# Fourier's first product over half the frequencies, modulation granules in pairs, angle steps in one place, and tensors moved to multiples of 128 bytes

## The reference

```python
mod_l = silu_c @ w_mod[l] + b_mod[l]      # w_mod[l]: 1024 x 3072
mod_c = silu_cc @ w_mod[l] + b_mod[l]
sh_l, sc_l, g_l = jnp.split(mod_l, 3, axis=-1)
h_l = rmsnorm(x, norm_g[l]) * (1 + sc_l[:, None]) + sh_l[:, None]
```

```python
ang = positions.astype(jnp.float32)[..., None] * inv_freq
return jnp.cos(ang), jnp.sin(ang)
```

## Time and profile before

| | us |
|---|---|
| median of 3 runs | 1123.51 |
| lowest, highest | 1123.21, 1123.52 |
| the profiled execution, as a whole | 1121.75 |
| its span (first to last instruction) | 1119.9 |

### The profile page before, as it was taken

The page is one execution under the profiler, slowest core; times in us unless marked ns, Lnnn a source line. Parts: engine busy times, 40 slices in busy tenths (PEclk is TensorE's granted clock), DMA queues, the critical chain, the costliest instruction groups (busy, mean ns, idle before and its releaser), DMA issues.

```text
span 1119.9 us, 15597 instructions
## 1 busy us (share of the span) xinstructions
PE 1086.1 (97%) x5974; PEld 883.6 (79%) x5974; DVE 683.9 (61%) x1198; ACT 554.7 (50%) x999; POOL 77.2 (7%) x94
## 2 busy tenths in 40 slices
PE   7999999999999999999999999999998999999997
PEld 5889776688886988776688778889796678889785
DVE  5986665566545786575566547523256753876664
ACT  5654364455435554364455445334235642534772
POOL 1000110000002000110000000001000002021040
PEclk9999999999999999999999999999999999999999
DMA  9644576665666744486876485223211012443001
GB/s 300 218 141 151 173 241 192 219 211 186 188 188 203 242 139 152 143 280 211 256 235 183 153 323 153 73 87 107 75 58 57 1 57 57 132 142 122 2 1 38
DMA packets 109716, 170.46 MB, mean 152 GB/s; under 512 B 7229, under 2 KB 70730, under 8 KB 109386
## 3 DMA queue, kind: packets, MB, share of 16 engines
q1 hardware_dynamic: 107668, 161.95, 45.8%
q0 software_dynamic: 1440, 6.10, 1.6%
q10 hardware_dynamic: 534, 1.41, 0.3%
HBM read 168.39 MB, written 1.05 MB: 151 GB/s over the span
## 4 chain that ended last, share of the span: by engine, by line
PE 84%; DVE 8%; ACT 4%; issue 3%; DMA 1%; POOL 0%; SPq 0%; DVEq 0%; POOLq 0%; ACTq 0%
PE PS L477 16%; PE PS L478 15%; PE PS L479 15%; PE PS L2997 4%; PE PS L2998 4%; PE PS L2999 4%; PE PS L977 3%; PE PS L1810 1%; DVE low L450 1%; PE PS L941 1%; PE PS L942 1%; PE PS L943 1%; PE PS L1484 1%; ACT high L440 1%; PE PS L1798 1%
## 5 line engine op out<-in xcount | busy, mean ns | idle before, releaser
L450 DVE TENSOR_TENSOR low<-raw,high 128x1024 fp32r<-128x1024 f32 (+3 forms) x182 | 202.2, 1116 | 190.8 <-ACT high L440 189.9
L477 PE MATMUL PS<-high,hT_high 128*128 128x512 f32 (+2 forms) x796 | 308.0, 387 | 4.3 <-DVE low L450 2.0
L478 PE MATMUL PS<-low,hT_high 128*128 128x512 f32 (+2 forms) x796 | 299.5, 376 | 0.0
L479 PE MATMUL PS<-high,hT_low 128*128 128x512 f32 (+2 forms) x796 | 299.4, 376 | 0.0
L440 ACT ACTIVATE high<-raw 128x1024 fp32r<-128x1024 f32 (+3 forms) x186 | 179.6, 972 | 221.1 <-PE PS L479 123.4
L477 PEld LDWEIGHTS PS<-high,hT_high 128*128 128x128 f32 x796 | 150.6, 189 | 49.5 <-issue 15.0
L453 DVE SCALAR_TENSOR_TENSOR low<-raw,vec_cols,high 128x512 fp32r<-128x512 f32 x176 | 124.2, 747 | 75.3 <-ACT high L443 75.2
L479 PEld LDWEIGHTS PS<-high,hT_low 128*128 128x128 f32 x796 | 150.5, 189 | 24.2
L478 PEld LDWEIGHTS PS<-low,hT_high 128*128 128x128 f32 x796 | 150.8, 189 | 21.7
L443 ACT ACTIVATE high<-raw,vec_cols 128x512 fp32r<-128x512 f32 x176 | 117.1, 714 | 73.9 <-PE PS L479 38.5
L2997 PE MATMUL PS<-high,fT_high 128*128 128x512 f32 x176 | 70.4, 400 | 0.0
(11 more groups left out here) (377 smaller groups left out, 1602.0 us busy)
## 6 DMA issues: line engine op xcount, KB each, us to landing
raw<-w_gate_up SPq DMA_DIRECT2D x176, 256.0 KB
raw<-w_mod SPq DMA_DIRECT2D x48, 512.0 KB
raw<-w_down SPq DMA_DIRECT2D x44, 512.0 KB
raw<-w_in SPq DMA_DIRECT2D x56, 384.0 KB
raw<-o_w_in SPq DMA_DIRECT2D x20, 512.0 KB
raw<-w_out SPq DMA_DIRECT2D x16, 512.0 KB
raw<-e_w_in SPq DMA_DIRECT2D x12, 512.0 KB
raw<-w_in SPq DMA_DIRECT2D x8, 512.0 KB
```

Source lines behind the costliest of these rows:

```text
L450: last = e.tensor_tensor(g.low, g.raw, g.high.bitcast(F32), ALU.subtract)
L477: e.matmul(bank, xh[:, k, tokens], g.high[:, i, :], start=first and i == 0, stop=False)
L478: e.matmul(bank, xh[:, k, tokens], g.low[:, i, :], start=False, stop=False)
L479: done = e.matmul(bank, xl[:, k, tokens], g.high[:, i, :], start=False, stop=last and i == len(g.rows) - 1)
```

## The change

Four edits, with no common core.

1. The token matrix keeps 129 of the 256 frequencies (0 to 128), for cosine and sine. The first product is 258 columns wide instead of 512. The copy out of PSUM becomes two: frequencies 0 to 127 as they stand, and 128 to 255 from 128 down to 1, read backwards. The sine part has the wrong sign there, so the second product takes the channel sines with the other sign for the upper tile (a third block of `dft_channels`).
2. `MOD_AT` names two places per chunk, h = 1 and h = 3, with two granules each.
3. The angle steps 5, 1 and 2 all come behind the cut of granule 3.
4. `hT_high` and `hT_low` are declared right behind `low`, and `half_power` is 8 columns wider. By the declared sizes both then start at a multiple of 128, and so does everything from `mixer` on.

```diff
-    parts["dft_tokens"] = by_tile(np.concatenate([np.cos(turn), np.sin(turn)], 1))
+    half = slice(0, SEQ // 2 + 1)
+    parts["dft_tokens"] = by_tile(np.concatenate([np.cos(turn)[:, half], np.sin(turn)[:, half]], 1))
...
-    parts["dft_channels"] = np.concatenate([np.cos(turn), -np.sin(turn)], 1) / np.sqrt(SEQ * P)
+    parts["dft_channels"] = np.concatenate([np.cos(turn), -np.sin(turn), np.sin(turn)], 1) / np.sqrt(SEQ * P)
...
         low = [sb(f"low{i}", [P, SLOT], F32R) for i in range(CUT)]
+        hT_high = sb("hT_high", [P, DK, SEQ], F32R)
+        hT_low = sb("hT_low", [P, DK, SEQ], F32R)
         consts = sb("consts", [P, a["const_early"].shape[1]])
...
-        hT_high = sb("hT_high", [P, DK, SEQ], F32R)
-        hT_low = sb("hT_low", [P, DK, SEQ], F32R)
...
-        half_power = sb("half_power", [P, 16])
+        half_power = sb("half_power", [P, 24])
...
-        MOD_AT = {(2, h): (0, h) for h in range(4)} | {(4, h): (1, h) for h in range(4)}
+        MOD_AT = {(2, 1): (0, 0), (2, 3): (0, 2), (4, 1): (1, 0), (4, 3): (1, 2)}
...
-                        add_mod(layer, 0, (of,), PAIRS[n:n + 1])
+                        add_mod(layer, 0, (of,), PAIRS[n:n + 2])
...
-                    last = e.matmul(PS[:, 4 + i % 4, :], z_late[:, NT * s + t, g * P:(g + 1) * P],
+                    last = e.matmul(PS[:, 4 + i % 4, 0:2 * FH], z_late[:, NT * s + t, g * P:(g + 1) * P],
                                     late_const("dft_tokens", NT)[:, t, :], start=t == 0, stop=t == NT - 1)
...
-                copy(e, mine, fourier_T[:, i, :], PS[:, 4 + i % 4, :]).then_inc(mine.sem, mine.mark(f"fourier{i}"))
+                halves = PS[:, 4 + i % 4, 0:2 * FH].rearrange("p (c n) -> p c n", c=2)
+                to = fourier_T[:, i, :].rearrange("p (c n) -> p c n", c=2)
+                copy(e, mine, to[:, :, 0:P], halves[:, :, 0:P])
+                copy(e, mine, to[:, :, P:SEQ], halves[:, :, P:0:-1]).then_inc(mine.sem, mine.mark(f"fourier{i}"))
...
+                        of = part * (1 + t % NT)
                         rows = slice(part * SEQ + t % NT * P, part * SEQ + (t % NT + 1) * P)
                         last = e.matmul(PS[:, F_BANKS[t], g * P:(g + 1) * P], fourier_T[:, 4 * s + g, rows],
-                                        channels[:, part * P:(part + 1) * P], start=part == 0, stop=part == 1)
+                                        channels[:, of * P:(of + 1) * P], start=part == 0, stop=part == 1)
...
-        EARLY = {0: 5, 1: 1, 2: 2, 4: 3, 6: 4}
+        EARLY = {0: (5, 1, 2), 4: (3,), 6: (4,)}
...
-                    early_dve(e, EARLY[s])
+                    for step in EARLY[s]:
+                        early_dve(e, step)
...
-                        mod_rows_pe(e, 0, of, slice(n, n + 1))
+                        mod_rows_pe(e, 0, of, slice(n, n + 2))
```

More of the change, by code:

```diff
@@ L1472, in program @@
                    for s, banks in enumerate(banks2))
+        FH = SEQ // 2 + 1
         def fourier_first_pe(e):
```

## The result

The changed kernel takes 1095.64 us, the median of four runs (1094.57 to 1096.27). The kernel before, run beside it on the same chip, took 1123.36 (1121.22 to 1123.52). The ratio is 0.9757, with a 95% interval from 0.974 to 0.9773. The forecast was 1106.9 with a range down to 1103.0, so the kernel is 11.3 us faster than forecast and 7.4 us outside the range.

A forecast was written before the change was run, and what follows sets the result against it. PE, busy 97% of the span, bounds the kernel. Savings of 9.36 (modulation pairs), 6.8 (Fourier), 0.44 (angles) and 0 (places) sum to 16.6 us, taken off 1123.51 for 1106.9 us, range 1103 to 1112.

The forecast's parts named there:

- Pairs: Modulation in gate_up: 16 single granules at 1.18 us become 8 pairs at 1.19, saving 9.36 us.
- price of a pair: Two modulation granules together cost PE 1.19 us, read from the last layer's down product; one alone costs 1.18.
- cover of 2.8 us: Slack in gate_up's chunk 3 between a buffer's release and cuts (6.8 us) and PE's use of the granule (9.6).
- "ring late" rival: Weight buffers given back in twos delay loads; half the modulation gain, 4.7 us, is lost, giving 1111.6; chance 8%.
- Fourier: First Fourier product: 32 instructions, each 254 columns narrower at 0.84 ns per column, save 6.8 us; copies cost 0.
- bound of twice the price for a backward read: Fourier's copies: were PSUM twice as slow backwards, DVE's pair would take 1.1 us, under PE's 1.74, costing nothing.
- Angles: Early angle steps fill DVE's idle time, so PE's product after its 2.71 us wait for `qk` starts 0.44 us sooner.
- the 1.4 us of that rival: PE's clock stays up behind the shortened `qk` wait, saving 1.4 us more, giving 1105.5; chance 27%.
- the wait of 2.02 us: A PE wait elsewhere in the earlier trace without a clock fall, cited as a sign the clock may stay up.
- Places of the tensors: Operand places in rounded products: rows show no dependence on place, so gain 0, with 0.233 us from start to start.
- every rounded product gets faster: Aligned operands cut rounded products from 0.457 to 0.417 ns per column, 20 ns per 512 columns, near 1045 us; chance 5%.
- Slower than before: Streaming and stationary operands at the same offset make reads meet; at 10 ns per 512-column product, 1133 us; chance 2%.

The follow-up runs named there:

- e2_no_places: The changed kernel with the new places of the tensors undone, so pairs, 129 frequencies and early angles alone: 1106.93 us beside 1122.82 for the kernel before, ratio 0.9859.
- e1_places: The kernel before with only the new tensor places added (`hT_high`, `hT_low` behind `low`, `half_power` wider): 1111.51 us beside 1122.82, ratio 0.9903.
- e11_fourier512: The changed kernel with all 256 frequencies in the first product and one copy per unit again: 1101.66 us beside 1122.11 for the kernel before.

## Why the prediction was wrong

**Pairs: right, and the ring a little late.** The sum of 9.36 holds (9.44 seen), and with it the price of a pair. But PE has one new wait for a low part, of 0.4 to 1.7 us, in every trace with pairs but those with the constants later. The prediction had named such a wait as a sign of being wrong, but looked for it in another place. Its cover of 2.8 us was worked out for the second granule of the chunk behind a pair (chunk 3), and PE doesn't wait there. The late granule is the second of chunk 4, whose load stands in SP's queue behind the next pair. And the forecast had counted the buffers and not the other loads: a large one on POOL's queue falls into the same stretch, in the second layer only. The "ring late" rival was right in kind at 1.7 of its 4.7 us.

**Fourier: right.** 0.217 per product and 6.8 us, copies at nothing. The bound of twice the price for a backward read wasn't needed: it takes 0.41 us where a forward one takes 0.42.

**Angles: the size right, the place not.** 0.4 to 0.5 for the 0.44, and ACT's table load was indeed late next. But the prediction took the 0.44 off the wait of 2.71 and expected 2.3. The wait is 2.64; five sixths of the gain lie at the product near 41 us that no longer comes late. The clock fell in this trace; behind the same wait it stayed up in others (granted 1.00 in e2_no_places), so the 1.4 us of that rival belong to every kernel here, before included. The prediction also leaned on the wait of 2.02 us in the earlier trace rows that isn't followed by a fall. In 5 of the 17 traces that same wait is.

**Places of the tensors: wrong, and the whole miss.** The time from start to start, which the prediction had named as its sign, went from 0.233 to 0.227. The step that failed says that "the costs would have to agree by accident", and concluded 0. It compared 397 ns (512 columns) with 280 (256 columns), took the 0.457 ns per column between them as the price of a column, and argued that a misplaced operand couldn't be in it, as it is the streaming one in the first and the stationary one in the second. But what counts is the distance between the two, and that was 32 bytes in both rows (with the roles exchanged), so comparing them could say nothing about it. The misplacement even had opposite signs in the two, and both went into the slope: it made 512 columns 6 ns longer and 256 columns 3 ns shorter. After the change the same two rows give (391 - 283) / 256 = 0.422 ns per column. The 0.04 ns above a cycle at 2.4 GHz, which the prediction saw and took for a property of the type, was the misplacement.

The rows of before could have warned. Here they are for the three widths, with the group of 384 that the prediction didn't use, groups by shape of the kernel before:

```profile
L478 PE MATMUL PS<-low,hT_high 128*128 128x384 f32 x252 | 85.3, 339 | 0.0
```

280, 339 and 397 lie on one line of 0.457 ns per column. Those are durations, whose ends are modelled. From start to start the same three take 118, 174 and 234 ns, steps of 56 and 60 for 128 columns each; after the change they take 120, 174 and 227, steps of 54 and 53. So the starts, which the prediction used elsewhere, put 512 columns off the line. No product of `high` or `low` with `hT`, `fT` or `cT` has a distance of 0 in the kernel before, so its trace couldn't say that the place was free. The words "no dependence on place" were read from rows in which the good place never occurred. The bounds for this step were 0 and the 20 ns per product of the rival, and the chance of 5% was too low for the only explanation it had of a slope above a cycle.

**The rival "every rounded product gets faster"** had the right mechanism in its slope (0.417 against the 0.422 seen) and the wrong size: 53 us and 10 more, where the kernel gained 11.3. It took the fixed part of a product as unchanged. By the durations it rose as the slope fell: 280 - 256 x 0.457 = 163 ns before, 283 - 256 x 0.422 = 175 after. So 256 columns lose 3 ns, 384 stay about even (339 to 337), and only 512 win, 6 ns in 397. The 2,592 such products by 5.6 ns (the mean spacing went from 233.2 to 227.6) are 14.5 us. About 1.0 of it is taken by the 256-column products (408 by 2.4 ns), 0.3 lies in the first 58 us, where PE waits for loads and cuts, and 0.7 goes into the longer wait near 528. Laid over each other, e2_no_places and the changed kernel drift apart by 11.7 us from 60 us to the end, so some 0.8 us stay unexplained.

**The rule on alignment.** The Trainium skill, "SBUF — State Buffer", section "Operand start alignment", asks for multiples of the element size. The prediction used it beside the step that failed. It tells what may be addressed; the time depends on more, 0.234 against 0.227 us for distances that are all allowed. The Trainium skill, "TensorE: Matmul & The Clock Gate", section "Wait — 56ns, not 53.3ns?", gives 215.7 ns for 512 columns, and its reading as a rival ("something to win back in every product") had the right sign. Here 227 is the lowest seen for this type; where the remaining 11 ns are, no run shows.

**Slower than before.** This rival had feared that the same offset makes reads meet. The 256-column products are the only ones where the new places cost something that counts, 0.120 against 0.118.

## What to carry to other kernels

Where a matrix product runs back to back, work out the cost per column from several widths; if it is above one cycle, try the distance between the streaming and the stationary tensor (modulo 256 bytes) before anything else, since it is a free edit. Don't take a dependence to be absent when every row has the same value of what would have to vary. When two buffers are given back at once, count the other queues' loads in that stretch too, and expect that a few microseconds won from a wait may not show in the median.

## What the runs showed of the hardware that I had not expected

- Rounded float32 products of 512 columns start 0.227 us apart when the two operands' start addresses differ by a multiple of 256 bytes, and 0.231 to 0.237 when they are off by 32, 64, 128, 160 or 224 (distances by the declared sizes). Absolute places don't matter (all at 32 past: 0.227).
- Narrower products hardly show it. 384 columns: 0.173 to 0.174 at distances of 0 and 32 on `hT`, 0.176 at 64 and 0.175 at 128, and 0.175 to 0.177 on `cT` at 160 and 224. 256 columns: 0.119 to 0.120 at a distance of 0, and 0.117 to 0.119 at the others but one (0.120 on `cT` at 160).
- A product is slow both for its own misplaced stationary operand and for that of the product behind it (234 and 232 ns against 227).
- The products that are full float32 don't show it: 512 columns start 0.429 us apart with `kT` and `qT`, whose distance is 0 in every layout, and 0.428 to 0.429 in the first Fourier product of before, e1_places and e11_fourier512, whose operands are at 0 in none of them. The two aren't the same product, so this is a comparison and no experiment.
- PSUM read backwards by DVE and ACT costs nothing visible: a forward and a backward copy of 256 take 0.76 on DVE and 0.66 on ACT, and alone 0.42 and 0.41 on DVE, 0.38 and 0.38 on ACT.
- Behind the same PE wait of 2.0 us the clock fell in 5 of 17 traces, which cost 1.7 us each time. Behind that of 2.4 to 2.7 us in the first 50 us it fell in 9 of 17, which cost 1.4 us. The two shortest of these waits (2.38 and 2.44 us) weren't followed by a fall, and those from 2.60 to 2.71 went either way, so the length of the wait doesn't decide it.
